# First block's attention with the values of two heads side by side and the reciprocals of the sums spread by transposes

## The chip, the core and the metric

The kernel runs on one core of one Trainium2 chip. The metric is the device time of one execution in microseconds (us), as the median of several. A core has a matrix engine (TensorE, PE in the profile; PEld are its weight loads), a vector engine (VectorE, DVE), a scalar engine (ScalarE, ACT), GpSimd (POOL) and an engine that issues transfers (SyncE, SP). Each engine works through its own queue in order, and they wait for each other through semaphores.

## What is computed

Two blocks, one after the other, on an input of 256 rows by 1024. The first is a recurrent layer, an MLP, an attention layer and another MLP. The second is a layer with a neighbourhood attention and two convolution branches. The change is in the attention of the first block alone. Cut to what matters:

```python
q, c, qi, ki, wi = jnp.split(h @ w_in, ATT_IN_SPLITS, axis=-1)
c = rms_norm(c, kv_norm_g)
...
_, idx = lax.top_k(score, topk)            # 64 of 256 keys for each query
logits = jnp.einsum('bqhc,bqkc->bqhk', q_lat_b, c_sel) + bias
p = jax.nn.softmax(logits, axis=-1)        # 16 heads
o_lat = jnp.einsum('bqhk,bqkc->bqhc', p, c_sel)
o = jnp.einsum('bshc,hcv->bshv', o_lat, w_uv).reshape(B, S, H_ATT * D_V)
return o @ w_o
```

## The kernel before, in words

**Staging.** Activations are kept transposed, features on the 128 partitions and 256 rows of the sequence on the free axis. Every weight is split into a high part (`wh`, made by ACT in `highs`, L276) and a low part (`wl`, made by DVE in `lows`, L283), and each activation too (`xh`, `xl`; here `oh`, `ol`). A product is three matmuls for each 128 of the inner dimension (L316, L318, L320): high with high, low with high, high with low. The logits, the exponentials and the values are plain fp32. For those the profile has two records for each matmul of the program (transposes have one).

**Attention.** The 256 queries are two blocks of 128. The first sees keys 0 to 127, the second all 256, so a head has 128 + 256 = 384 columns of logits (`SPANS`). Selection is a mask that GpSimd adds to the position bias (`bm`). Heads come in 8 pairs `m`, heads 2m and 2m+1. The loop over `k` is a software pipeline, written out by hand for each engine in its own function, and its order sets the order of every queue:

- `tensor_logits` (L1133, PE): the two heads of a pair side by side in rows 0 to 63 and 64 to 127 of the array.
- `vector_logits` (L1275, DVE): adds the mask and bias out of PSUM and finds the row's extreme, four instructions with four reads of the accumulator for a pair.
- `scalar_exp` (L1392, ACT): exponentials in place, the sum of each row as a by-product into `SM`.
- `tensor_flip` (L1142, PE): three 128x128 transposes for a head, so that keys come to the partitions; `scalar_flip` (L1385, ACT) copies them into `pt0` or `pt1`.
- `tensor_values` (L1153 to L1155, PE): for each head three matmuls whose stationary operand is a 128x128 piece of `pt` and whose moving operand is the head's 64 columns of values `VV`. The result has queries on the partitions.
- `vector_values` (L1281, L1286, DVE): reciprocal of the pair's four columns of sums, and the product into `os`.
- `tensor_outputs` (L1162, PE): two transposes bring heads to the partitions; `scalar_outputs` (L1397, ACT) makes `oh`, `vector_outputs` (L1292, DVE) makes `ol`.

Pair m has its logits in step m, flips and values in step m + 1, and outputs in step m + 2. Between these PE does products that don't depend on them: the second half of the query projections (`QSTEPS`, 12 matmul groups or 24 in a step) and then parts of the output projection (`tensor_wo`). In a step ACT makes one high part when `n` of `QSTEPS` is even (steps 0, 1, 3 and 5), DVE one low part in each of steps 0 to 7.

## Time and profile before

| | |
|---|---|
| median of 3 runs | 850.02 us (849.93 to 850.28) |
| the profiled execution | 849.28 us, span of the core 847.5 us |
| TensorE busy | 842.2 us, 99% of the span |
| VectorE busy | 647.2 us, 76% |
| ScalarE busy | 505.9 us, 60% |
| the loop over pairs | about 311.8 to 353.3 us of the span |

The span is the stretch that the profile shows; 1.8 us of the profiled execution lie outside it. The busy time of an engine is an average over stages and tells nothing of a single wait. Matmul records overlap, so PE's busy share can be full while it is not at its peak; what a group of matmuls costs is read from the start of its first record to the start of what follows.

### The profile page before, as it was taken

Reading aid. Unit: us, or ns where it says so; the run is one execution under the profiler, and the core shown is the slowest. Engines: PE = TensorE matmul, PEld = TensorE weight load, DVE = VectorE, ACT = ScalarE, POOL = GpSimd, SP = SyncE. Lnnn points to the kernel's source line nnn. Section 1 sums busy time; section 2 is a strip of 40 time slices with the busy share of each in tenths; the row PEclk is TensorE's granted clock in tenths of the full one; section 3 lists DMA queues with packets and bytes.
Section 4 is the critical chain, followed back from the end, with each engine's and each line's share of the span. In section 5 each row is a group of like instructions: output and inputs, shape, how many; then the busy total and the mean of one; then the engine's idle time right before and its main releaser. Section 6 shows DMA issues by size and latency. Waiting matters only on the chain.

```text
span 847.5 us, 17537 instructions
## 1 busy us (share of the span) xinstructions
PE 842.2 (99%) x7184; PEld 822.4 (97%) x7184; DVE 647.2 (76%) x1229; ACT 505.9 (60%) x925; POOL 46.8 (6%) x63
## 2 busy tenths in 40 slices
PE   8999999999999999999999999999999999999998
PEld 7999999999999998999999999999999999999998
DVE  6978668898987697586667555566699889998873
ACT  5795777774435567578878444434456685444650
POOL 0000000000000127100000000021020000000000
PEclk9999999999999999999999999999999999999999
DMA  9927868788887824177757865526564424556541
GB/s 300 347 70 224 276 213 264 265 281 267 299 263 233 283 72 140 51 247 237 208 174 217 242 207 189 189 71 154 172 198 151 148 77 142 156 170 192 170 144 50
DMA packets 162865, 164.23 MB, mean 194 GB/s; under 512 B 16816, under 2 KB 159328, under 8 KB 162528
## 3 DMA queue, kind: packets, MB, share of 16 engines
q1 hardware_dynamic: 161696, 162.05, 60.6%
q8 instruction: 57, 0.93, 0.5%
q10 hardware_dynamic: 1088, 1.05, 0.4%
q14 instruction: 24, 0.20, 0.1%
HBM read 162.01 MB, written 2.91 MB: 195 GB/s over the span
## 4 chain that ended last, share of the span: by engine, by line
PE 97%; DVE 1%; DMA 1%; ACT 0%; SPq 0%; POOL 0%; issue 0%
PE ps L316 25%; PE ps L318 25%; PE ps L320 25%; PE ps L442 3%; PE ps L1594 2%; PE ps L1592 2%; PE ps L1596 2%; PE ps L459 2%; PE ps L1685 1%; PE ps L1687 1%; PE ps L1689 1%; PE ps L1643 1%; PE ps L1654 1%; PE ps L1634 1%; DMA raw<-in_rec_w_in_dram 1%; PE ps L1133 1%
## 5 line engine op out<-in xcount | busy, mean ns | idle before, releaser
L283 DVE TENSOR_TENSOR wl<-raw,wh 128x1024 fp32r<-128x1024 f32 x256 | 309.1, 1223 | 27.1 <-ACT wh L276 27.0
L316 PE MATMUL ps<-xh,wh 128*128 128x256 f32 x1136 | 319.1, 281 | 0.0
L318 PE MATMUL ps<-xl,wh 128*128 128x256 f32 x1136 | 315.1, 277 | 0.0
L320 PE MATMUL ps<-xh,wl 128*128 128x256 f32 x1136 | 315.0, 277 | 0.0
L276 ACT ACTIVATE wh<-raw 128x1024 fp32r<-128x1024 f32 x256 | 267.1, 1051 | 73.7 <-PE ps L320 66.0
L316 PEld LDWEIGHTS ps<-xh,wh 128*128 128x128 f32 x1136 | 213.3, 188 | 3.1 <-issue 1.2
L318 PEld LDWEIGHTS ps<-xl,wh 128*128 128x128 f32 x1136 | 213.8, 188 | 0.4 <-DVE xl L384 0.2
L320 PEld LDWEIGHTS ps<-xh,wl 128*128 128x128 f32 x1136 | 213.8, 188 | 0.0
L320 PE MATMUL ps<-hh,wl 128*128 128x256 f32 x512 | 141.3, 276 | 0.0
L316 PE MATMUL ps<-hh,wh 128*128 128x256 f32 x512 | 141.3, 276 | 0.0
L318 PE MATMUL ps<-hl,wh 128*128 128x256 f32 x512 | 141.3, 276 | 0.0
L316 PEld LDWEIGHTS ps<-hh,wh 128*128 128x128 f32 x512 | 96.1, 188 | 0.0
L318 PEld LDWEIGHTS ps<-hl,wh 128*128 128x128 f32 x512 | 96.1, 188 | 0.0
L320 PEld LDWEIGHTS ps<-hh,wl 128*128 128x128 f32 x512 | 96.1, 188 | 0.0
L864 DVE TENSOR_TENSOR hl<-tmp,hh 128x256 fp32r<-128x256 f32 x64 | 27.2, 426 | 41.1 <-ACT tmp L857 40.8
L1826 DVE SCALAR_TENSOR_TENSOR ca<-up,sb_vec,ca 128x256 f32<-128x256 f32 x120 | 50.9, 479 | 0.0
L852 ACT ACTIVATE tmp<-ps 128x256 f32<-128x256 f32 x64 | 24.2, 379 | 26.2 <-PE ps L320 26.2
L884 DVE SCALAR_TENSOR_TENSOR aw<-aw,cb 128x1024 f32<-128x1024 f32 x24 | 29.3, 1220 | 6.0 <-DMA aw<-in_w_adaT_dram 5.9
L390 ACT ACTIVATE xh<-x,sb_vec 128x256 fp32r<-128x256 f32 x24 | 12.2, 510 | 34.5 <-DVE x L380 34.4
L442 PE MATMUL ps<-xg,raw 128*128 128x256 f32 x128 | 29.0, 382 | 1.5 <-DMA raw<-in_rec_w_in_dram 0.9
L442 PEld LDWEIGHTS ps<-xg,raw 128*128 128x128 f32 x128 | 23.8, 190 | 5.4 <-DMA raw<-in_rec_w_in_dram 1.7
L854 ACT ACTIVATE hh<-tmp 128x256 fp32r<-128x256 f32 x64 | 26.8, 419 | 2.0
(365 smaller groups left out, 1396.4 us busy)
## 6 DMA issues: line engine op xcount, KB each, us to landing
raw<-in_w_in_dram SPq DMA_DIRECT2D x34, 1024.0 KB, 5.4
raw<-in_mlp_up_dram SPq DMA_DIRECT2D x32, 1024.0 KB, 5.5
raw<-in_mlp_down_dram SPq DMA_DIRECT2D x32, 1024.0 KB, 7.1
aw<-in_w_adaT_dram SPq DMA_DIRECT2D x24, 512.0 KB, 4.7
raw<-in_rec_w_in_dram SPq DMA_DIRECT2D x7, 1024.0 KB, 11.6
raw<-in_att_w_in_dram SPq DMA_DIRECT2D x6, 1024.0 KB, 5.5
raw<-in_rec_w_out_dram SPq DMA_DIRECT2D x4, 1024.0 KB, 5.9
raw<-in_att_w_o_dram SPq DMA_DIRECT2D x4, 1024.0 KB, 5.0
```

The lines of the kernel that those rows point to most:

```text
L276: e.activation(parts_of(i)[0], raw_of(i), ACT.Copy).then_inc(S["wh"], 1)
L283: e.tensor_tensor(parts_of(i)[1], raw_of(i), f32(parts_of(i)[0]), op=ALU.subtract).then_inc(S["wl"], 1)
L316: e.matmul(o, H[:, first + n], xh[:, k], start=start and n == 0, stop=False)
L318: e.matmul(o, H[:, first + n], xl[:, k], start=False, stop=False)
L320: ins = e.matmul(o, L[:, first + n], xh[:, k], start=False, stop=stop and n == len(ks) - 1)
L442: ins = e.matmul(o, w[:, k], XG[:, k], start=k == 0, stop=k == 7)
L459: ins = e.matmul(o, RIW[:, n, m, j, 128 * (t % 2):128 * (t % 2) + 128], XC[:, 2 * n + j], start=j == 0, stop=j == 1)
L852: e.activation(r[:], ps[f"up{l}.{f}"], ACT.Relu).then_inc(S["hr"], 1)
L854: e.activation(HH[l][:, f], r[:], ACT.Square).then_inc(S["hh"], 1)
L864: e.tensor_tensor(HL[l][:, f], TM.of[f"s{l}.{f}"][0][:], f32(HH[l][:, f]), op=ALU.subtract).then_inc(S["hl"], 1)
L884: e.scalar_tensor_tensor(PAIR[:] if src else AW[n % 2][:], AW[n % 2][:], 1.0, CB[:, src], op0=ALU.mult, op1=ALU.mult, accum_out=(ADC if sr ...
L1826: e.scalar_tensor_tensor(CA[:, t], UP[:, t, j:j + 256], w, CA[:, t], op0=ALU.mult, op1=ALU.add).then_inc(S["cf"], 1)
```

## The change

It does four things.

1. Values: the head's 64 columns of `VV` become the stationary operand and the flipped exponentials the moving one, 256 columns for the first 128 keys and 128 for the others. The two heads of a pair go to the lower and the upper 64 partitions of one PSUM tile, so four matmuls stand in place of six, and the result has head dimensions on the partitions already. The exponentials of both heads now lie in one tile `PT` and are copied out of two PSUM banks by one ACT instruction of 768 columns.
2. Division: since queries now lie along the free axis, the reciprocals have to lie there too. DVE writes them as a tile `RR1` of 128x256 (`vector_ratios`: each of the four columns of sums is read 64 times by a stride of zero), PE transposes it with two 128x128 transposes (`tensor_ratios`), ACT copies the result into `RX` (`scalar_ratios`), and DVE multiplies (`vector_divided`) into `OT`. The transposes of the outputs are gone.
3. High and low parts of the output are made from `OT` in SBUF in place of PSUM.
4. The pipeline is a step deeper: flips of pair m in step m + 2, values, ratios and outputs in step m + 3. Both flips of a pair stand ahead of the logits. The loop has 11 steps, the pieces of the output projection beside it (`WO_BESIDE`) are laid out anew, and DVE makes its low part at the end of a step.

On DVE, in step 3, this stands before (the pair's reciprocal and product, the logits of heads 6 and 7, then the low parts; `ps` is PSUM, `small` holds the sums):

```order
L1281 RECIPROCAL small_84<-small_84 128x4
L1286 TENSOR_TENSOR os1_134<-ps2,small_84 128x256
L1275 ISA sx2_118,small_84<-ps4,bm0_131 128x128
L1275 ISA small_84 128x1
L1275 ISA sx2_118,small_84<-ps4,bm0_131 128x256
L1275 ISA small_84 128x1
L1275 ISA sx3_119,small_84<-ps5,bm1_132 128x128
L1275 ISA small_84 128x1
L1275 ISA sx3_119,small_84<-ps5,bm1_132 128x256
L1275 ISA small_84 128x1
L1292 TENSOR_TENSOR ol_136<-ps3,oh_135 128x256
L283 TENSOR_TENSOR wl0_62<-raw3_54,wh0_56 128x1024
```

and now:

```order
L1290 TENSOR_TENSOR ot0_132<-ps0,rx0_138 128x256
L1283 RECIPROCAL rr11_137<-small_84 128x256
L1276 ISA sx2_118,small_84<-ps4,bm0_130 128x128
L1276 ISA small_84 128x1
L1276 ISA sx2_118,small_84<-ps4,bm0_130 128x256
L1276 ISA small_84 128x1
L1276 ISA sx3_119,small_84<-ps5,bm1_131 128x128
L1276 ISA small_84 128x1
L1276 ISA sx3_119,small_84<-ps5,bm1_131 128x256
L1276 ISA small_84 128x1
L1294 TENSOR_TENSOR ol_135<-ot0_132,oh_134 128x256
L283 TENSOR_TENSOR wl0_62<-raw3_54,wh0_56 128x1024
```

The reciprocal is now 128x256 in place of 128x4. It still stands ahead of the four logits instructions, and so does the product, which now belongs to a pair one step older and reads `rx`, a copy that ACT makes.

On ACT, steps 3 to 4, this stands before (flips, outputs, four exponentials, the high part of a weight, and the next flip):

```order
L1385 ACTIVATE pt0_120<-ps67 128x384
L1385 ACTIVATE pt1_121<-ps67 128x384
L1397 ACTIVATE oh_135<-ps3 128x256
L1392 ACTIVATE sx2_118,small_84<-sx2_118,small_84 128x128
L1392 ACTIVATE sx2_118,small_84<-sx2_118,small_84 128x256
L1392 ACTIVATE sx3_119,small_84<-sx3_119,small_84 128x128
L1392 ACTIVATE sx3_119,small_84<-sx3_119,small_84 128x256
L276 ACTIVATE wh3_59<-raw4_55 128x1024
```

and now:

```order
L1408 ACTIVATE oh_134<-ot0_132 128x256
L1403 ACTIVATE sx2_118,small_84<-sx2_118,small_84 128x128
L1403 ACTIVATE sx2_118,small_84<-sx2_118,small_84 128x256
L1403 ACTIVATE sx3_119,small_84<-sx3_119,small_84 128x128
L1403 ACTIVATE sx3_119,small_84<-sx3_119,small_84 128x256
L276 ACTIVATE wh3_59<-raw4_55 128x1024
L1390 ACTIVATE pt_120<-ps67 128x768
L1396 ACTIVATE rx1_139<-ps2 128x256
L1408 ACTIVATE oh_134<-ot1_133 128x256
```

The copy `rx`, for which DVE's product waits, stands behind the exponentials of the step before, the high part and the wide copy `pt`; and `oh` waits for DVE's product.

The diff, cut:

```diff
@@ -1013,7 +1013,7 @@
     RT = [place(f"rt{i}", [128, 384], at=at_t) for i in range(2)]
     at_s = [ARENA]
     SX = [place(f"sx{i}", [128, 384], at=at_s) for i in range(4)]
-    PT = [place(f"pt{i}", [128, 384], at=at_s) for i in range(2)]
+    PT = place("pt", [128, 2, 384], at=at_s)
     at_t = [max(at_t[0], at_s[0])]
     SC = place("score", [128, 384], at=at_t)
     MK = place("mask", [128, 384], at=at_t)
@@ -1026,18 +1026,23 @@
     at_q = at_t[0]
     Q = place("q", [128, 8, 256], at=at_t)
     BM = [place(f"bm{i}", [128, 384], at=at_t) for i in range(2)]
-    OS = [place(f"os{i}", [128, 2, 128], at=at_t) for i in range(2)]
+    OT = [place(f"ot{i}", [128, 256], at=at_t) for i in range(2)]
     OH = place("oh", [128, 8, 256], F32R, at=[at_q])
     OL = place("ol", [128, 8, 256], F32R, at=at_t)
+    RR1 = [place(f"rr1{i}", [128, 256], at=at_t) for i in range(2)]
+    RX = [place(f"rx{i}", [128, 256], at=at_t) for i in range(2)]
     BT = place("bt", [128, 16, 256], at=[HALF])
     RQ, CVAR, CRS = TINY[:, 4:6], TINY[:, 6:8], TINY[:, 8:10]
     WI = SMALL[:, 0:16]
     M8 = [SMALL[:, 16 + 8 * i:24 + 8 * i] for i in range(2)]
-    MN, SM, RC = (SMALL[:, 32 + 32 * i:64 + 32 * i] for i in range(3))
+    MN, SM = (SMALL[:, 32 + 32 * i:64 + 32 * i] for i in range(2))
     SPANS = ((0, 128), (128, 384))
     QI_AT = {3: 1, 0: 2, 1: 3, 2: 4}
     SCORES = [2 * j + hh for j in (3, 0, 1, 2) for hh in range(2)]
     QSTEPS = (0, 0, 1, 2, 3, 4, 5, 6)
+
+    WO_BESIDE = {7: ((0, 0, 4),), 8: ((1, 0, 5),), 9: ((2, 0, 6), (0, 4, 6)),
+                 10: ((3, 0, 6), (1, 5, 7), (0, 6, 7), (2, 6, 7), (3, 6, 7))}
 
 
     def tensor_x2(e, q, name, *freed):
@@ -1136,7 +1141,7 @@
                     ins.then_inc(closing(f"lg{2 * m + i}", p[i]), 1)
 
     def tensor_flip(e, q, h):
-        p = claim(q, AUX[2 + h % 2], (S["pt"], h + 1))
+        p = claim(q, AUX[2 + h % 2], (S["pt"], h // 2 + 1))
         q.wait_ge(S["ex"], 2 * h + 2)
         for i in range(3):
             ins = e.matmul(p[:, i * 128:(i + 1) * 128], SX[h % 4][:, i * 128:(i + 1) * 128], ident, is_transpose=True)
@@ -1144,23 +1149,24 @@
 
     def tensor_values(e, q, m):
 
-        p = claim(q, AUX[m - 6], (S["os"], m + 1)) if m > 5 else main(q, (S["os"], m + 1))
+        p = claim(q, AUX[(m - 5) % 2], (S["ot"], m + 1)) if m > 4 else main(q, (S["ot"], m + 1))
         q.wait_ge(S["vv"], 4)
-        for i in range(2):
-            h, pt = 2 * m + i, PT[i]
-            cols, a, b = slice(64 * h, 64 * h + 64), slice(64 * i, 64 * i + 64), slice(128 + 64 * i, 192 + 64 * i)
-            q.wait_ge(S["pt"], h + 1)
-            e.matmul(p[:, a], pt[:, 0:128], VV[:, 0, cols], start=True, stop=True)
-            e.matmul(p[:, b], pt[:, 128:256], VV[:, 0, cols], start=True, stop=False)
-            e.matmul(p[:, b], pt[:, 256:384], VV[:, 1, cols], start=False, stop=True).then_inc(
-                closing(f"val{h}", p[:, 0:256]), 1)
-
-    def tensor_outputs(e, q, m):
-        p = claim(q, AUX[0], (S["ol"], 8)) if m == 7 else main(q, (S["ol"], m + 1))
-        q.wait_ge(S["os"], m + 1)
+        q.wait_ge(S["pt"], m + 1)
+        for blk, (lo, hi) in enumerate(((0, 256), (256, 384))):
+            for i in range(2):
+                h = 2 * m + i
+                ins = e.matmul(p[64 * i:64 * i + 64, 128 * blk:256], VV[:, blk, 64 * h:64 * h + 64], PT[:, i, lo:hi],
+                               start=blk == 0, stop=blk == 1)
+        ins.then_inc(closing(f"val{m}", p), 1)
+
+    def tensor_ratios(e, q, m):
+
+        p = ps[f"val{m}"]
+        q.wait_ge(S["rc"], m + 1)
         for blk in range(2):
-            ins = e.matmul(p[:, blk * 128:blk * 128 + 128], OS[m % 2][:, blk], ident, is_transpose=True)
-        ins.then_inc(closing(f"heads{m}", p[:, 0:256]), 1)
+            ins = e.matmul(p[:, 256 + 128 * blk:384 + 128 * blk], RR1[m % 2][:, 128 * blk:128 * blk + 128], ident,
+                           is_transpose=True)
+        ins.then_inc(closing(f"heads{m}"), 1)
 
     def tensor_wo(e, q, f, lo, hi):
 
@@ -1174,29 +1180,24 @@
         for m in range(4):
             for half in range(2):
                 tensor_q(e, q, m, half)
-        for k in range(10):
-            if 1 <= k < 9:
-                tensor_flip(e, q, 2 * k - 2)
+        for k in range(11):
+            if k > 2:
+                tensor_values(e, q, k - 3)
+            if 2 <= k < 10:
+                tensor_flip(e, q, 2 * k - 4)
+                tensor_flip(e, q, 2 * k - 3)
+            if k > 2:
+                tensor_ratios(e, q, k - 3)
             if k < 8:
                 tensor_logits(e, q, k)
-            if 1 <= k < 9:
-                tensor_flip(e, q, 2 * k - 1)
-            if k == 9:
-                tensor_wo(e, q, 0, 5, 7)
-                tensor_wo(e, q, 1, 6, 7)
-            if k > 1:
-                tensor_outputs(e, q, k - 2)
             for n, step in enumerate(QSTEPS):
                 if step == k:
                     tensor_q(e, q, 4 + n // 2, n % 2)
-            if k in (7, 8):
-                tensor_wo(e, q, k - 7, 0, k - 2)
-            if 1 <= k < 9:
-                tensor_values(e, q, k - 1)
-        tensor_wo(e, q, 2, 0, 7)
-        for f in range(3):
+            for f, lo, hi in WO_BESIDE.get(k, ()):
+                tensor_wo(e, q, f, lo, hi)
+        for f in range(4):
             tensor_wo(e, q, f, 7, 8)
-        for f in range(3, 8):
+        for f in range(4, 8):
             tensor_wo(e, q, f, 0, 8)
 
 
@@ -1275,21 +1276,22 @@
             e.tensor_tensor_reduce(SX[h % 4][:, lo:hi], ps[f"lg{h}"][:, lo:hi], BM[h % 2][:, lo:hi], 1.0, 3e38,
                                    ALU.add, ALU.min, MN[:, 2 * h + blk:2 * h + blk + 1]).then_inc(S["lg"], 1)
 
-    def vector_values(e, q, m):
-        rc = RC[:, 4 * m:4 * m + 4]
+    def vector_ratios(e, q, m):
         q.wait_ge(S["ex"], 4 * m + 4)
-        e.reciprocal(rc, SM[:, 4 * m:4 * m + 4]).then_inc(S["rc"], 1)
-        q.wait_ge(S["rc"], m + 1)
-        q.wait_ge(S["mm"], done[f"val{2 * m + 1}"])
         if m > 1:
             q.wait_ge(S["mm"], done[f"heads{m - 2}"])
-        e.tensor_tensor(OS[m % 2][:].rearrange("p a (h d) -> p (a h) d", h=2),
-                        ps[f"val{2 * m}"].rearrange("p (s d) -> p s d", s=4),
-                        rc.unsqueeze(2).to_broadcast([128, 4, 64]), op=ALU.mult).then_inc(S["os"], 1)
+        e.reciprocal(RR1[m % 2][:].rearrange("p (s d) -> p s d", s=4),
+                     SM[:, 4 * m:4 * m + 4].unsqueeze(2).to_broadcast([128, 4, 64])).then_inc(S["rc"], 1)
+
+    def vector_divided(e, q, m):
+        if m > 1:
+            q.wait_ge(S["ol"], m - 1)
+        q.wait_ge(S["rx"], m + 1)
+        e.tensor_tensor(OT[m % 2][:], ps[f"val{m}"][:, 0:256], RX[m % 2][:], op=ALU.mult).then_inc(S["ot"], 1)
 
     def vector_outputs(e, q, m):
         q.wait_ge(S["oh"], m + 1)
-        e.tensor_tensor(OL[:, m], ps[f"heads{m}"], f32(OH[:, m]), op=ALU.subtract).then_inc(S["ol"], 1)
+        e.tensor_tensor(OL[:, m], OT[m % 2][:], f32(OH[:, m]), op=ALU.subtract).then_inc(S["ol"], 1)
 
     def vector_attention(e, q):
         vector_latent(e, q)
@@ -1302,24 +1304,26 @@
         e.tensor_scalar(MK[:], SC[:], -2e38, -NEG, op0=ALU.is_ge, op1=ALU.mult).then_inc(S["mk"], 1)
         q.wait_ge(S["mk"], 1)
         e.scalar_tensor_tensor(MK[:], cc("causal"), -1.0, MK[:], op0=ALU.mult, op1=ALU.max).then_inc(S["mk"], 1)
-        for k in range(10):
+        for k in range(11):
+            if k > 2:
+                vector_divided(e, q, k - 3)
+            if 2 <= k < 10:
+                vector_ratios(e, q, k - 2)
             if k < 8:
                 vector_logits(e, q, 2 * k)
                 if k == 0:
                     vector_q(e, q, 1)
                 vector_logits(e, q, 2 * k + 1)
-            if k > 1:
-                vector_outputs(e, q, k - 2)
-            if k < 8:
-                lows(e, q, at["q5"] + k + 1)
+            if k > 2:
+                vector_outputs(e, q, k - 3)
             if k == 0:
                 vector_q(e, q, 2)
                 vector_q(e, q, 3)
             for n, step in enumerate(QSTEPS):
                 if step == k and n % 2:
                     vector_q(e, q, 4 + n // 2)
-            if 1 <= k < 9:
-                vector_values(e, q, k - 1)
+            if k < 8:
+                lows(e, q, at["q5"] + k + 1)
         for f in range(8):
             q.wait_ge(S["mm"], done[f"wo{f}"])
             x_add(e, q, 2, f, ps[f"wo{f}"])
@@ -1378,11 +1382,18 @@
             q.wait_ge(S["mm"], done[f"vv{n}"])
             e.activation(VV[:, n // 2, 512 * (n % 2):512 * (n % 2) + 512], ps[f"vv{n}"], ACT.Copy).then_inc(S["vv"], 1)
 
-    def scalar_flip(e, q, h):
-        q.wait_ge(S["mm"], done[f"flip{h}"])
-        if h > 1:
-            q.wait_ge(S["mm"], done[f"val{h - 2}"])
-        e.activation(PT[h % 2][:], ps[f"flip{h}"], ACT.Copy).then_inc(S["pt"], 1)
+    def scalar_flip(e, q, m):
+
+        q.wait_ge(S["mm"], done[f"flip{2 * m + 1}"])
+        if m:
+            q.wait_ge(S["mm"], done[f"val{m - 1}"])
+        e.activation(PT[:], PAIR[:].rearrange("p (b c) -> p b c", b=2)[:, :, 0:384], ACT.Copy).then_inc(S["pt"], 1)
+
+    def scalar_ratios(e, q, m):
+        q.wait_ge(S["mm"], done[f"heads{m}"])
+        if m > 1:
+            q.wait_ge(S["ot"], m - 1)
+        e.activation(RX[m % 2][:], ps[f"val{m}"][:, 256:512], ACT.Copy).then_inc(S["rx"], 1)
 
     def scalar_exp(e, q, h):
         for blk, (lo, hi) in enumerate(SPANS):
@@ -1393,19 +1404,19 @@
                          accum_out=SM[:, at_sum:at_sum + 1]).then_inc(S["ex"], 1)
 
     def scalar_outputs(e, q, m):
-        q.wait_ge(S["mm"], done[f"heads{m}"])
-        e.activation(OH[:, m], ps[f"heads{m}"], ACT.Copy).then_inc(S["oh"], 1)
+        q.wait_ge(S["ot"], m + 1)
+        e.activation(OH[:, m], OT[m % 2][:], ACT.Copy).then_inc(S["oh"], 1)
 
     def scalar_attention(e, q):
         scalar_latent(e, q)
         for m in range(4):
             highs(e, q, ahead(f"q{m}")[0])
-        for k in range(10):
-            if 1 <= k < 9:
-                scalar_flip(e, q, 2 * k - 2)
-                scalar_flip(e, q, 2 * k - 1)
-            if k > 1:
-                scalar_outputs(e, q, k - 2)
+        for k in range(11):
+            if 2 <= k < 10:
+                scalar_flip(e, q, k - 2)
+            if k > 2:
+                scalar_ratios(e, q, k - 3)
+                scalar_outputs(e, q, k - 3)
             if k < 8:
                 scalar_exp(e, q, 2 * k)
                 scalar_exp(e, q, 2 * k + 1)
```

## Rows read from the trace of the kernel before

**Rows 1.** The page: busy times, TensorE's clock, and the chain that ended last.

```profile
PE 842.2 (99%) x7184; PEld 822.4 (97%) x7184; DVE 647.2 (76%) x1229; ACT 505.9 (60%) x925; POOL 46.8 (6%) x63
...
PEclk9999999999999999999999999999999999999999
...
PE 97%; DVE 1%; DMA 1%; ACT 0%; SPq 0%; POOL 0%; issue 0%
```

**Rows 2.** Timeline, PE, one step (start us, us, engine, line, operation, tiles).

```profile
336.86 0.33 PE L1153 MATMUL ps<-vv,pt 128*128 128x64 f32 x2
...
341.42 0.33 PE L1153 MATMUL ps<-vv,pt 128*128 128x64 f32 x2
...
342.70 0.50 PE L1142 MATMUL ps<-sb_con,sx 128*128 128x128 f32 x3
343.13 0.93 PE L1133 MATMUL ps<-kk,q 64*128 64x128 f32 x8
343.98 0.55 PE L1142 MATMUL ps<-sb_con,sx 128*128 128x128 f32 x3
```

**Rows 3.** Timeline, PE, second block: values of two heads.

```profile
657.46 0.66 PE L1654 MATMUL ps<-pt,v 128*64 128x128 f32 x8
657.95 0.61 PE L1654 MATMUL ps<-pt,vc 128*64 128x128 f32 x8
658.48 1.09 PE L1643 MATMUL ps<-sb_con,s 128*128 128x128 f32 x8
```

**Rows 4.** Groups by form, DVE: reciprocals and two neighbours (xcount | busy, mean ns | idle).

```profile
L1902 DVE RECIPROCAL small<-small 128x2 f32<-128x2 f32 x8 | 1.3, 158 | 0.0
L1281 DVE RECIPROCAL small<-small 128x4 f32<-128x4 f32 x8 | 1.3, 165 | 0.0
L490 DVE RECIPROCAL small<-small 128x8 f32<-128x8 f32 x1 | 0.2, 203 | 0.0
...
L488 DVE TENSOR_SCALAR small<-small 128x8 f32<-128x8 f32 x1 | 0.2, 172 | 0.3 <-ACT small L704 0.3
...
L1286 DVE TENSOR_TENSOR os<-ps,small 128x256 f32<-128x256 f32 x8 | 3.4, 425 | 5.2 <-PE ps L1155 5.0
```

**Rows 5.** Timeline, DVE, step 4 of the pairs.

```profile
330.39 0.29 DVE L1275 CUSTOM_DVE_ANT_0 sx<-ps,bm 128x128 f32<-128x128 f32 x1 [0.69 <-PE ps L1133]
...
331.51 0.08 DVE L1275 DVE_READ_ACCUMULATOR2_ANT small<- 128x1 f32 x1
331.68 0.42 DVE L1292 TENSOR_TENSOR ol<-ps,oh 128x256 fp32r<-128x256 f32 x1
332.01 1.33 DVE L283 TENSOR_TENSOR wl<-raw,wh 128x1024 fp32r<-128x1024 f32 x1
333.27 0.41 DVE L1267 TENSOR_TENSOR q<-ps,rs 128x256 f32<-128x256 f32 x1
```

**Rows 6.** Timeline, ACT, step 3; then two of its groups by form.

```profile
326.94 0.40 ACT L1392 ACTIVATE sx<-sx,small 128x128 f32<-128x128 f32 x1
...
328.70 1.04 ACT L276 ACTIVATE wh<-raw 128x1024 fp32r<-128x1024 f32 x1
329.64 0.47 ACT L1385 ACTIVATE pt<-ps 128x384 f32<-128x384 f32 x1
...
L2116 ACT ACTIVATE pt<-ps 128x512 f32<-128x512 f32 x16 | 8.7, 594 | 9.5 <-PE ps L1643 9.4
L1385 ACT ACTIVATE pt<-ps 128x384 f32<-128x384 f32 x16 | 7.7, 488 | 9.0 <-PE ps L1142 8.9
L1397 ACT ACTIVATE oh<-ps 128x256 fp32r<-128x256 f32 x8 | 3.0, 381 | 4.2 <-PE ps L1162 4.2
```

**Rows 7.** Timeline, PE: the two halves of q4, and the last transposes.

```profile
312.88 0.28 PE L318 MATMUL ps<-xl,wh 128*128 128x256 f32 x1
...
315.38 0.28 PE L320 MATMUL ps<-xh,wl 128*128 128x256 f32 x1
...
353.12 0.38 PE L1162 MATMUL ps<-sb_con,os 128*128 128x128 f32 x2
```

More of the change, by code:

```diff
@@ L93, in hybrid_two_block_kernel @@
         "y yh yl eb silu hr hh hsq hl dn ada cnd qi ki wt rq wi c csq cvar crs ch cl rt sc sel mk kk vv q bm lg "
[1 row of a table removed]
-        "sa scz cgt cv by bb bz byz ybh ybl cf lsum lc lsq lacc lnv lnr rsl ly lt lq ych ycl "
[1 row of a table added]
+        "sa scz cgt cv by bb bz byz ybh ybl cf lsum lc lsq lacc lnv lnr rsl ly lt ych ycl "
         "lg2 ex2 pt2 rc2 nm2 bh yam yah yal gt mg mt mh ml fx"
```

2 rows, old and new, of the table S are left out of this document.

## The prediction

> **What bounds the kernel now.** I read the page first. PE is busy for 842.2 of 847.5 us, 97% of the chain that ended last is PE's, and the granted clock is at full speed in all slices [rows 1]. So the time is PE's queue from end to end, and only two things can change it: what PE's own instructions take, and waits that do not exist today. Next I read PE's timeline of one step of the loop over pairs. The reader is to see there that each group starts where the former ends, with no idle time noted: six matmuls of values from 341.42 to 342.70, a flip, the logits from 343.13 to 343.98, the other flip [rows 2]. A step takes 4.56 us, from the values at 336.86 to the next at 341.42 [rows 2]. DVE and ACT follow PE: DVE's logits wait 0.69 us for PE each time [rows 5]. Last I read DVE's and ACT's timelines, because the change moves work onto them.
>
> **What the change saves on PE.** The values of a pair take 342.70 - 341.42 = 1.28 us [rows 2]. The new form, 64 stationary columns and two heads in two halves of the array, is not in this loop, but the second block has it: 16 records, two by two, four pairs of records with 128 moving columns in 657.95 - 657.46 = 0.49 us, the next four in 0.53 [rows 3], so 0.12 to 0.13 us for a pair of records. The new values of a pair of heads are two pairs of records with 256 columns and two with 128, together six such units: 0.74 to 0.79 us. The logits, two heads in two halves of the rows, consist of the same number of records and columns and take 343.98 - 343.13 = 0.85 us with their switch [rows 2]. I take 0.79. The saving is 0.49 us for each pair of heads. Against it stand switches of layout. Eight transposes span 1.09 us, of which the last one's own record is some 0.3, so 0.11 each [rows 3], and three flips with the switch to the logits take 0.43 [rows 2]: a switch costs 0.1 us. One more stands now ahead of the values and one behind them, and the logits are now left towards products. I charge 0.15 to 0.2 us for a step, which leaves 0.3 us for each of eight pairs, 2.5 us in all; PE's full step becomes 4.25 us. Flips (48) and the other transposes (16) keep their number. If the two heads did not overlap, the values would cost 1.5 us and all of this would be lost; rows 3 speak against it.
>
> **What it adds: one term decides.** DVE's reciprocal goes from 128x4 to 128x256. No row shows that size. The bounds: from below, a DVE instruction of 256 columns, 0.43 us [rows 4]. From above, reciprocals by their own rows: 158 ns at 2 columns, 165 at 4, 203 at 8, while a tensor_scalar of 8 columns takes 172 [rows 4]. From 2 to 8 columns that is 45/6 = 7.5 ns a column, where ordinary instructions gain 1.2 (1.33 us at 1024 columns, 0.41 at 256 [rows 5]). From 4 to 8 it is 9.5. So R, the time of one reciprocal, is 158 + 254 x 7.5 = 2.06 us, at most 165 + 252 x 9.5 = 2.56, at least 0.43. The evidence is thin: one record of 203 ns carries the slope, and 165 at 4 columns would fit ordinary speed. I still take R = 2.05, because the steep slope is in instructions of the very same operation. The Trainium skill, "VectorE: DVE Perf Modes", section "First, the fixed hardware budget", says that a reciprocal is an iterated divide with a repeat count of 8; read as 8 cycles of its 0.96 GHz a column it would give an estimate of 2.3 us for R and by the sum below about 858 us. The trace's 7.5 ns a column agrees with it nearly.
>
> **Where R lands.** DVE's own work for a step would be the product 0.34, R, four logits instructions 1.12, low part of the output 0.34, a projection every other step 0.17, the low part of a weight 1.26 [rows 5]: 5.2 us against PE's 4.25. But a longer loop is closed through ACT. Reciprocal, then the first logits instruction, then ACT's four exponentials, its high part, the wide copy `pt`, the copy `rx`, then DVE's product, and the next reciprocal behind it. In numbers: R less an overlap of 0.08, 1.97; first logits instruction 0.30 [rows 5]; four exponentials 328.70 - 326.94 = 1.76; `pt` of 768 columns from 488 ns at 384 and 594 at 512, so 0.83 ns a column and 0.81 us, 0.70 from start to start; `rx` 0.38 by the 381 of `oh`, the same shape from PSUM [rows 6]; product 0.34; two handovers of 0.03. Sum 5.5 us, and 0.94 more (329.64 - 328.70 [rows 6]) in steps with a high part. PE cannot run ahead of it: its logits wait for DVE's of the step before, its transposes for the reciprocal, and its values for `pt`.
>
> **The sum.** Reciprocal of pair 0 starts: the last matmul of q4 ends at 315.38 + 0.28 = 315.66 [rows 7]; DVE then makes q4 (0.34), the low part (1.26), the logits of step 1 (1.12), the low part (1.26) [rows 5], so 319.7 us, no sooner than PE's logits of step 2. From there to the reciprocal of pair 6 are six rounds, two of them (steps 3 and 5) with a high part: 6 x 5.5 + 2 x 0.94 = 34.9, so 354.6. It ends at 356.65. PE, which waits for it, then does two transposes (0.22), the 24 products beside step 9 and the values of pair 7 (0.88 with the switch). Products take (315.38 - 312.88)/22 = 0.1136 us each [rows 7], so 2.73. The transposes of pair 7 start near 360.5, where today the last ones start at 353.12 [rows 7]: 7.4 us later. Behind them PE has 141 products of the output projection left, today 150: 9 x 0.1136 = 1.0 us less. Net 6.4 us, less at most 0.2 for rounding of handovers: I say 6.3. The low part of pair 7 is ready some 2 us before the products that use it, so that adds nothing. Behind the loop PE's queue is unchanged and full, so the delay is passed to the end whole. The profiled execution would go from 849.28 to 855.6 us; it is 0.7 below the median of 850.02, against which I forecast 850.0 + 6.3 = 856.3 us. Each 0.1 us of R is worth 0.7 us, seven reciprocals in line.
>
> **What I cost at nothing.** The reciprocal of the last pair and the two passes from `OT`: in steps 9 and 10 they lie beside PE's products. `RX` and `OT` as such: ACT and DVE have the time when R is small. GpSimd's bias additions are made for a pair while DVE is at the one before; should DVE's longer instruction hold GpSimd up, I allow up to 2 us in all, which the steeper case below holds. PE's waits are spread over six rounds, some 1.5 us in each, so I expect no fall of the clock, as there is none now [rows 1].
>
> **Rivals.** *The reciprocal runs at the pace of other DVE instructions* (R = 0.43). The loop is then 3.9 us, 4.8 with a high part, against PE's 4.25; some 0.3 us of waiting are left, the PE saving of 2.5 stands, 847.6 us. For it: 165 ns at 4 columns and one sole record at 8. It decides below R of about 1.1 us, where what the rounds add equals what PE saves. The Trainium skill, the same page, section "The TRN2 errata — SBUF-src ops pay a fixed extra latency per instruction", has a cycle table with 58 cycles and one for each element for VectorE; taken for the reciprocal that is an estimate of 0.33 us and this rival's time, and no row of a reciprocal above 8 columns is there to refuse it. *In between* (R from 0.7 to 1.4, say because only a start-up is slow): the loop eats what PE saves, 849 to 851.5, no change. *Steeper or with contention*: R = 2.56 by the slope from 4 to 8, or GpSimd and DVE hold each other up: 3.5 us more, 860. *The heads don't overlap in the array*: with the slow reciprocal only 0.4 us more, since PE waits anyway; with the fast one 850 to 854. Its entry in rows 3 is so clear that I give it 2 in 100.
>
> **Numbers.** Slow reciprocal, R from 1.8 to 2.3, 70 in 100, by itself 853.5 to 858.5. Steeper or contention 8 (858.5 to 861). Fast 16, in between 6. A measurement of this kernel tells about 0.2%, 1.7 us, from no change: faster takes 13 from the fast case, same gets 3 + 6, slower the rest, 78. The range from 849.0 to 859.5 holds the slow case, half of the steeper one and the one in between, 80 in 100; it leaves out the fast one.
>
> **What would show it.** Reciprocals of 128x256 at 2.0 to 2.1 us; their starts 5.5 and 6.4 us apart; PE idle ahead of the logits for DVE, ahead of the transposes for the reciprocal and ahead of the values for `pt`, some 9 us in all between 320 and 361; the values at 0.79 us with records two by two; the last transposes near 360.5. The forecast is wrong if the reciprocal takes 0.43 us, and off by size if the rounds are set by something else than ACT's queue.

## The result, and the profile after

The changed kernel takes 856.94 us in the median of four executions (856.56 to 857.46); the kernel before took 850.15 us beside it (849.93 to 850.99). The ratio is 1.0078, with a 95% interval of 1.0063 to 1.0093: it is slower by 6.8 us. The forecast was 856.3. The profiled execution is the slowest of the four, 857.46 us, with a span of 855.7 us, 8.2 more than before.

The page, against [rows 1]:

```profile
PE 845.0 (99%) x7152; PEld 819.8 (96%) x7152; DVE 658.7 (77%) x1229; ACT 508.6 (59%) x925; POOL 46.9 (5%) x63
...
PE 91%; DVE 5%; ACT 2%; issue 1%; DMA 1%; POOL 0%; ACTq 0%; DVEq 0%
```

PE is still busy for 99% of the span, but of the chain that ended last DVE and ACT now have 7%, where they had 1%. DVE gained 11.5 us of work. The timeline of DVE shows where, against [rows 5] (start us, us; in brackets the idle time before and who ended it):

```profile
334.09 1.42 DVE L283 TENSOR_TENSOR wl<-raw,wh 128x1024 fp32r<-128x1024 f32 x1
335.57 0.42 DVE L1290 TENSOR_TENSOR ot<-ps,rx 128x256 f32<-128x256 f32 x1
335.91 1.74 DVE L1283 RECIPROCAL rr<-small 128x256 f32<-128x256 f32 x1
...
338.96 1.75 DVE L283 TENSOR_TENSOR wl<-raw,wh 128x1024 fp32r<-128x1024 f32 x1
341.71 0.43 DVE L1290 TENSOR_TENSOR ot<-ps,rx 128x256 f32<-128x256 f32 x1 [1.00 <-ACT rx L1396]
342.05 1.74 DVE L1283 RECIPROCAL rr<-small 128x256 f32<-128x256 f32 x1
```

The reciprocal takes 1.74 us. From 335.91 to the next at 342.05 it is 6.14 us, and the product waits 1.00 us for `rx`. ACT's timeline of the same round, against [rows 6]:

```profile
339.61 1.05 ACT L276 ACTIVATE wh<-raw 128x1024 fp32r<-128x1024 f32 x1
340.56 0.78 ACT L1390 ACTIVATE pt<-ps 128x768 f32<-128x768 f32 x1
341.25 0.36 ACT L1396 ACTIVATE rx<-ps 128x256 f32<-128x256 f32 x1
```

The last exponential starts at 339.12; high part, `pt` and `rx` follow it without a gap, and DVE's product starts 0.1 us after `rx` ends. That is the closed round of the forecast, in the order in which it was written down. It is closed through ACT where a high part is in it; in the shorter rounds, like the one that starts at 330.71, DVE's product has no idle time before it. PE's timeline, against [rows 2]:

```profile
330.21 0.87 PE L1158 MATMUL ps<-pt,vv 128*64 128x256 f32 x8 [0.16 <-ACT pt L1390]
331.02 0.88 PE L1147 MATMUL ps<-sb_con,sx 128*128 128x128 f32 x6
332.51 0.44 PE L1167 MATMUL ps<-sb_con,rr 128*128 128x128 f32 x2 [0.62 <-DVE rr L1283]
333.65 0.93 PE L1138 MATMUL ps<-kk,q 64*128 64x128 f32 x8 [0.71 <-DVE small L1276]
...
336.08 0.87 PE L1158 MATMUL ps<-pt,vv 128*64 128x256 f32 x8
...
345.67 1.05 PE L1138 MATMUL ps<-kk,q 64*128 64x128 f32 x8 [1.38 <-DVE q L1268]
...
358.59 0.44 PE L1167 MATMUL ps<-sb_con,rr 128*128 128x128 f32 x2
```

PE waits for `pt` (0.2 us in all), for the reciprocal (1.3) and for DVE's logits (1.4), the three that were named. A fourth wait was not named and is the longest single one: 1.38 us before the last logits, for the last projection `q`, which DVE makes behind the reciprocal and the logits of its step. A step from values to values is 336.08 - 330.21 = 5.87 us in place of 4.56. The last transposes stand at 358.59, where they stood at 353.12 [rows 7]: 5.5 us later. Nine products fewer stand behind them, so the loop itself costs 4.4 us.

The rest of the time is lost behind the loop, where the forecast had nothing. In the kernel before, DVE's first and last addition to `x` after the output projection, and PE's product of the row statistics (L333), which comes behind the first products of the MLP:

```profile
356.28 0.42 DVE L380 TENSOR_TENSOR x<-x,ps 128x256 f32<-128x256 f32 x1 [1.90 <-PE ps L320]
...
370.87 0.42 DVE L380 TENSOR_TENSOR x<-x,ps 128x256 f32<-128x256 f32 x1
```

```profile
373.20 0.28 PE L333 MATMUL ps<-sb_con,sqa 128*128 128x2 f32 x2
```

In the changed kernel, DVE and then PE:

```profile
363.17 0.42 DVE L380 TENSOR_TENSOR x<-x,ps 128x256 f32<-128x256 f32 x1 [2.28 <-PE ps L320]
...
375.56 0.41 DVE L380 TENSOR_TENSOR x<-x,ps 128x256 f32<-128x256 f32 x1
...
377.76 0.41 DVE L380 TENSOR_TENSOR x<-x,ps 128x256 f32<-128x256 f32 x1
```

```profile
374.87 0.28 PE L316 MATMUL ps<-xh,wh 128*128 128x256 f32 x1
...
377.56 0.39 PE L318 MATMUL ps<-xl,wh 128*128 128x256 f32 x1 [0.38 <-DVE xl L384]
...
378.77 0.38 PE L316 MATMUL ps<-xh,wh 128*128 128x256 f32 x1 [0.70 <-ACT xh L390]
...
379.72 0.35 PE L333 MATMUL ps<-sb_con,sqa 128*128 128x2 f32 x2
```

DVE needs 2.20 us for each group of the output projection (377.76 - 375.56: the addition, a low part of a weight, the low part of `x`, its squares), and 14.59 us from the first addition to the last, in both kernels. PE's first product of the MLP comes 4.4 us later than before (370.48 there), but the first addition comes 6.9 us later, since four groups now end together behind the loop in place of three. So DVE's last `xl` is too late for PE, which waits twice, and the product of the statistics stands at 379.72, 6.5 us later than before.

The windows show the clock (us from:to, busy time, PEclk the granted clock):

```profile
340.00:346.00 6.00, 3.80 (x34) 2.93 (x34) 5.00 (x14) 4.04 (x13) 3.35 (x5) 1.00 0.03 9
346.00:350.00 4.00, 4.00 (x24) 3.20 (x22) 3.94 (x12) 2.04 (x7) 1.86 (x2) 0.57 0.44 129
376.00:380.00 4.00, 2.78 (x19) 2.08 (x17) 3.42 (x7) 2.61 (x6) 0.00 (x0) 1.00 0.84 261
380.00:384.00 4.00, 4.00 (x22) 4.00 (x22) 3.47 (x5) 2.86 (x5) 0.71 (x1) 0.57 0.53 140
```

Twice, right after stretches in which PE was busy for 3.80 of 6 and 2.78 of 4 us, TensorE is granted 1.2 in place of 2.4 GHz: a mean of 0.57 over 4 us is 3.4 us at half speed. The second time the queue is full. From this product of the statistics to the next of its kind PE takes 43.53 us (379.72 to 423.25), in the kernel before 41.92 (373.20 to 415.12): the half speed cost 1.6. So the profiled execution had lost 4.4 + 2.1 + 1.6 = 8.1 us here. Farther back it loses 1.1 us between 586 and 647 us and gets 1.0 back behind it; a kernel with the attention of before shows the same loss (e5, last section), so it is not put down to the change. The three other executions have a mean clock of 1.000, where this one has 0.996; their difference of 6.8 us to the kernel before is the first two terms, 6.5, and 0.3 left over. That they lost the same two terms is inferred: only one execution has a trace.

### The profile page after: what moved, and what is told of

Its sections match the earlier page's. It is cut to its first block, busy times and chain, and to the rows that moved or that the text cites. A ratio compares the mean times of both kernels' runs of the same rounds, so it can differ in the third digit from the quotient of the medians.

```text
span 855.7 us, 17472 instructions
## 1 busy us (share of the span) xinstructions
PE 845.0 (99%) x7152; PEld 819.8 (96%) x7152; DVE 658.7 (77%) x1229; ACT 508.6 (59%) x925; POOL 46.9 (5%) x63
## 4 chain that ended last, share of the span: by engine, by line
PE 91%; DVE 5%; ACT 2%; issue 1%; DMA 1%; POOL 0%; ACTq 0%; DVEq 0%
PE ps L316 24%; PE ps L318 24%; PE ps L320 24%; PE ps L442 2%; PE ps L1605 2%; PE ps L1607 2%; PE ps L1603 2%; PE ps L459 2%; PE ps L1696 1%; PE ps L1698 1%; PE ps L1700 1%; DVE wl L283 1%; PE ps L1665 1%; PE ps L1654 1%; PE ps L1645 1%
```

## The experiments

Four questions were open: whether the reciprocal is all that makes the loop slow; whether the rounds close through ACT; what the loss behind the loop is; and what the reciprocal costs by size. The last runs put the answers together.

**e1: the reciprocal stays small.** The changed kernel with DVE's spreading done by a multiplication.

```diff
-        e.reciprocal(RR1[m % 2], <4 columns of SM, each read 64 times>)
+        e.reciprocal(rc, SM[:, 4 * m:4 * m + 4])
+        e.tensor_scalar(RR1[m % 2], <4 columns of rc, each read 64 times>, 1.0, None, op0=ALU.mult)
```

> The changed kernel, but the reciprocal is taken of the four columns of sums (128x4) and a tensor_scalar by 1.0 spreads it to 128x256. Theory A, the 1.74 us reciprocal sets the rounds through ScalarE's queue: it becomes 0.17 + 0.35 us, the rounds fall from 5.2 and 6.1 us to 3.9 and 4.9, PE hardly waits between 320 and 360 us (under 1.5 us, now about 8), and the time is 847.5 to 849.0 us. Rival B, the deeper pipeline and the copy rx cost by themselves: it stays at 854 us or more.

Measured: 852.02 us (850.83 to 854.62), ratio 1.0032 (1.0020 to 1.0045) to 849.58. PE's timeline:

```profile
321.62 0.87 PE L1158 MATMUL ps<-pt,vv 128*64 128x256 f32 x8
...
325.87 0.87 PE L1158 MATMUL ps<-pt,vv 128*64 128x256 f32 x8
...
353.19 0.44 PE L1167 MATMUL ps<-sb_con,rr 128*128 128x128 f32 x2
...
374.31 0.35 PE L333 MATMUL ps<-sb_con,sqa 128*128 128x2 f32 x2
```

In the loop the theory holds: steps of 4.25 us, to the hundredth what the forecast gave PE alone, two waits of PE left (0.80 us for `q`, 0.42 for DVE's logits), and the last transposes at 353.19 in place of 358.59. But the total is 3 us over the range that was expected. PE's MLP starts a microsecond earlier than before, and the statistics 1.1 us later: the same loss of 2.1 us behind the loop as in the changed kernel. So that loss has nothing to do with the reciprocal, nor with a late loop. Of the seven executions four have a mean clock of 0.998 (spans 849.0, 851.2, 852.2, 852.7) and three of 1.000 (849.0, 849.7, 850.2); the profiled one is at half speed for 3.4 us around 376, behind these waits. From its statistics to the next of their kind it takes 44.78 us (to 419.09) in place of 41.92; the half speed explains 1.7 of these 2.9 us, the rest is a slower pace of the products with no wait between them (last section).

**e2: `rx` ahead of `pt` on ACT.** Nothing else is changed.

```diff
         for k in range(11):
-            if 2 <= k < 10:
-                scalar_flip(e, q, k - 2)
             if k > 2:
                 scalar_ratios(e, q, k - 3)
+            if 2 <= k < 10:
+                scalar_flip(e, q, k - 2)
+            if k > 2:
                 scalar_outputs(e, q, k - 3)
```

> The changed kernel, with ScalarE's small copy rx put ahead of its wide copy pt in each step; nothing else. Theory A, the round runs through ScalarE: it loses the 0.7 us of pt until VectorE's own work (4.9 us a step) holds it, so rounds of about 4.9 and 5.4 us in place of 5.2 and 6.1, some 2.5 us less in all, 854.0 to 855.0 us. Rival C, VectorE's own work or PE's waits for the reciprocal already set the pace: no change, 856.5 to 857.3.

Measured: 854.61 us (854.06 to 857.32), ratio 1.0067 (1.0055 to 1.0080). DVE's timeline:

```profile
334.72 1.74 DVE L1283 RECIPROCAL rr<-small 128x256 f32<-128x256 f32 x1
...
339.82 0.42 DVE L1290 TENSOR_TENSOR ot<-ps,rx 128x256 f32<-128x256 f32 x1 [0.31 <-ACT rx L1396]
340.17 1.74 DVE L1283 RECIPROCAL rr<-small 128x256 f32<-128x256 f32 x1
```

The round with a high part is 5.45 us in place of 6.14, the wait for `rx` 0.31 in place of 1.00: exactly the 0.69 by which `rx` stands earlier. The last transposes stand at 356.47, 2.1 us earlier, and of the 6.8 us by the medians 5.0 are left. That is inside the range expected if the round runs through ACT. The ratios alone would not show it, since their intervals overlap: two of the five executions have a mean clock of 0.998 and spans of 854.5 and 855.5 us, where the other three have 852.3 to 852.7. The trace does. The round closes through ACT where a high part is in it; in the others (5.06 us here, 5.20 in the changed kernel) DVE's product does not wait for `rx`, and DVE's own queue is the limit.

**e3: three groups beside the loop.** The output projection is divided as in the kernel before: groups 0, 1 and 2 beside the loop, five behind it.

```diff
-                 10: ((3, 0, 6), (1, 5, 7), (0, 6, 7), (2, 6, 7), (3, 6, 7))}
+                 10: ((1, 5, 7), (0, 6, 7), (2, 6, 7))}
...
-        for f in range(4):
+        for f in range(3):
             tensor_wo(e, q, f, 7, 8)
-        for f in range(4, 8):
+        for f in range(3, 8):
```

> The changed kernel, but with three groups of the output projection begun beside the loop (0, 1, 2) in place of four, as in the kernel before. Theory D, behind the loop VectorE needs 2.2 us for each of the eight groups and four groups that end together leave PE 2.7 us of products for only four more: PE then waits about 2 us at the start of the next MLP and the clock falls for 3.4 us there. With three groups these waits go, at the price of 0.7 us of waiting for the last low part: 853.5 to 855.5 us. Rival: PE's waits at 377 us come from the late loop itself and stay: 856.5 to 857.5.

Measured: 853.75 us (853.48 to 854.10), ratio 1.0049 (1.0036 to 1.0062). PE's timeline:

```profile
358.46 0.44 PE L1167 MATMUL ps<-sb_con,rr 128*128 128x128 f32 x2
...
378.17 0.28 PE L333 MATMUL ps<-sb_con,sqa 128*128 128x2 f32 x2
```

The loop ends where it ended (358.46), DVE's additions start 1.8 us earlier (361.36), both waits of PE are gone, and the statistics come 1.55 us earlier. It is not the whole 2.1, because the fourth group had covered something: with twelve products in place of 33 between the last transposes and those that read the last `oh` and `ol`, PE's weight loads wait 0.27 us for each of the two, and three products there take 1.03 us in the starts (360.01 to 361.04) in place of 0.34. The ratio falls by 0.0029, 2.5 us, a microsecond more than the trace says; the intervals allow both. Its profiled execution is granted half speed in the loop, near 346, and has a span of 851.7, as much as its sister executions with a mean clock of 1.000 (851.7 to 852.1): in the loop, where PE waits for DVE anyway, half speed shows no cost in the span.

**e4: the kernel before with a large reciprocal that nobody reads.** In `vector_values`, ahead of the small one.

```diff
+        e.reciprocal(RQX[m % 2], <4 columns of SM, each read 64 times>)
         e.reciprocal(rc, SM[:, 4 * m:4 * m + 4]).then_inc(S["rc"], 1)
```

> The kernel before, with a reciprocal of 128x256 into a tile that nobody reads, ahead of its own small one in each of the eight steps. VectorE's own work for a step goes from about 3.5 to 5.2 us against PE's 4.56. Theory A in its general form (1.7 us more on VectorE can't be hidden in this loop): PE waits about 0.6 us a step from step 2 on, 854 to 856 us. Rival (only the closed round through rx makes it costly): under 851.5 us.

Measured: 853.70 us (853.00 to 855.24), ratio 1.0050 (1.0037 to 1.0063). DVE and PE:

```profile
334.70 1.74 DVE L1282 RECIPROCAL rqx<-small 128x256 f32<-128x256 f32 x1
...
339.73 1.74 DVE L1282 RECIPROCAL rqx<-small 128x256 f32<-128x256 f32 x1
```

```profile
326.71 0.41 PE L1163 MATMUL ps<-sb_con,os 128*128 128x128 f32 x2 [0.62 <-DVE os L1289]
```

Eight of these instructions alone cost 4.1 us, just under the range expected and far over the rival's 851.5: DVE's round becomes 5.0 to 5.4 us by its own work, more than PE's 4.56, and PE waits for `os` in six of the eight steps, here 0.62 us. The last transposes stand at 356.85. With e1 this shows the cause of the loss in the loop from both sides: without the large reciprocal they stand where they stood (353.19 against 353.12), and the large reciprocal alone moves them by 3.7 us in a loop that has neither `rx` nor the deeper pipeline.

**e5: the reciprocal by size.** The kernel before with reciprocals of 2 to 128 columns and multiplications of 1, 32 and 223 at the head of DVE's queue, all reading one column by a stride of zero. The edit adds, in `vector_mixer`:

```diff
+        for n in (2, 4, 8, 16, 32, 64, 128):
+            e.reciprocal(SQX[:, at_p:at_p + n], NEGH[:, 0:1].to_broadcast([128, n]))
```

> The kernel before, with reciprocals of 128x2, 4, 8, 16, 32, 64 and 128, read with a stride of zero, and tensor_scalars of 128x1, 32 and 223 at the start of VectorE's queue, where it waits for the input. If every column costs the reciprocal 6.3 ns (1.744 us at 256), 128 columns take 0.94 us, 64 take 0.54 and 32 take 0.34, while 32 columns of tensor_scalar take 0.18. If instead the cost began only above some size, or came from the copies' three-dimensional pattern in the changed kernel, 128 columns would take 0.3 us.

Measured in one execution of 850.4 us, the groups of DVE (the number after the bar: busy us, mean ns):

```profile
L564 DVE RECIPROCAL sqx<-negh 128x128 f32<-128x128 f32 x1 | 0.9, 895 | 0.0
...
L564 DVE RECIPROCAL sqx<-negh 128x64 f32<-128x64 f32 x1 | 0.5, 495 | 0.0
...
L564 DVE RECIPROCAL sqx<-negh 128x32 f32<-128x32 f32 x1 | 0.3, 296 | 0.0
L567 DVE TENSOR_SCALAR tmp<-negh 128x223 f32<-128x223 f32 x1 | 0.3, 270 | 0.0
...
L564 DVE RECIPROCAL sqx<-negh 128x8 f32<-128x8 f32 x1 | 0.2, 174 | 0.0
...
L564 DVE RECIPROCAL sqx<-negh 128x4 f32<-128x4 f32 x1 | 0.2, 157 | 0.0
```

From 64 to 128 columns it is 400 ns, 6.25 ns a column; from 128 to 256, with the 1744 ns of the changed kernel, 849 ns, 6.6 a column. Up to 8 columns the time stays between 157 and 174 ns, so the slope can't be read there. The one record of 8 columns takes 174 ns here; the kernel's own, on which the forecast's slope hung, takes 203 in this run too. The expectation's rival, 0.3 us for 128 columns, is refuted.

**e8: e1 and e3 together**, and **e9: `rx` first as well** (the edits of e1, e3, and e2).

> Both remedies together: the reciprocal of 128x4 with a tensor_scalar that spreads it, and three groups of the output projection beside the loop. Theory: what is left of the change is PE's saving of about 0.3 us for a pair, less 0.8 us of waiting for q7, 0.4 for a free bank and 0.6 for the last low part: 848.5 to 850.0 us on this chip, no clear difference from before. Rival: if the deeper pipeline has a price of its own, or PE's saving is not there, 851 or more.

> As the run before it, and ScalarE's copy rx ahead of its copy pt. The rounds through ScalarE lose 0.7 us, so VectorE's q7 comes earlier and the wait of 0.8 us ahead of the last logits goes: 848.0 to 849.5 us, about 0.5 us under the run without it. If that wait has another cause: the same as without it.

Measured, beside 27 executions of the kernel before (850.08 us): e8 849.76 us (849.33 to 850.90), ratio 1.0001 (0.9992 to 1.0010); e9 848.46 us (847.73 to 848.94), ratio 0.9982 (0.9973 to 0.9990). All executions have a mean clock of 1.000. PE's timeline of e9:

```profile
352.04 0.44 PE L1167 MATMUL ps<-sb_con,rr 128*128 128x128 f32 x2
...
371.74 0.28 PE L333 MATMUL ps<-sb_con,sqa 128*128 128x2 f32 x2
```

e8 has its statistics at 373.12, where the kernel before has 373.20; e9 at 371.74, 1.5 us earlier, and the median follows with 1.6. So e9 is better than both kernels, by a little: of the 2.5 us that PE was to save in the loop 1.5 arrive. The last transposes stand 1.1 us earlier than before, with nine products (1.0 us) more ahead of them, so 2.1 us are saved in the loop, in steps of 4.26 us; 0.7 are lost again to the wait for the last `oh` and `ol`, as in e3. In e8 PE still waits 1.2 us at two places in the loop, for `q` (0.81) and for DVE's logits (0.42); with `rx` first those two are gone. By the medians e9 gains 1.3 us on e8, more than the 0.5 expected.

**e7: PE spreads the ratios itself**, with three groups as in e3, and **e10: `rx` first as well.** The tile `RR1` goes; four matmuls with 64 stationary columns, all the same column of the small reciprocal, stand in place of the two transposes, directly behind the values.

```diff
+            for i in range(2):
+                ins = e.matmul(p[64 * i:64 * i + 64, 256 + 128 * blk:384 + 128 * blk],
+                               RC[:, 4 * m + 2 * blk + i:4 * m + 2 * blk + i + 1].to_broadcast([128, 64]), ident,
+                               start=True, stop=True)
```

> Three groups beside the loop, and no spread tile at all: four matmuls with the column of reciprocals as a stationary operand of 64 equal columns and the identity moving, right behind the values, in place of two transposes. VectorE loses the 0.35 us of spreading, PE pays 4 pairs of records (0.44 us) for two transposes (0.22): 0.2 us more for a pair on PE. 848.5 to 850.5 us: a little better than the tensor_scalar if VectorE still sets the pace, a little worse (1 us) if PE does.

> The kernel of the run e7 (the reciprocals of the sums stay a column of four; four products of TensorE with the identity spread them; three groups of the output projection beside the loop) with ScalarE's copy of the spread ratios put ahead of its copy of the flipped exponentials. In e7 the part beside the loop and behind it costs TensorE 2.5 us less of gaps than in the changed kernel, and the last transposes lie where they lay before. Theory (the round through ScalarE still sets VectorE's and with it TensorE's step): the earlier copy takes 0.5 to 1.6 us off, as it did in e9 against e8 (1.3 us): 848.4 to 849.6 us. Rival (TensorE is already full in e7's loop, 39.92 us busy in 40 us, so no order of copies can give it anything): 849.8 to 850.2 us. Second rival: a difference of kernels of under 1 us is set by the stretch from 600 to 645 us, where every changed kernel so far came back 0.8 to 1.2 us late whatever was done in the loop; then it falls on e7's time as well.

Measured: e7 850.05 us (849.26 to 851.38), ratio 1.0001 (0.9992 to 1.0010); e10 849.95 us (849.31 to 850.61) beside 849.95, ratio 1.0002 (0.9993 to 1.0011). PE's timeline of e7:

```profile
330.45 0.87 PE L1158 MATMUL ps<-pt,vv 128*64 128x256 f32 x8
331.16 0.61 PE L1168 MATMUL ps<-sb_con,small 128*64 128x128 f32 x8
331.69 0.87 PE L1147 MATMUL ps<-sb_con,sx 128*128 128x128 f32 x6
...
334.96 0.87 PE L1158 MATMUL ps<-pt,vv 128*64 128x256 f32 x8
```

A step is 4.51 us, 0.25 more than in e9 and nearly the 4.56 of before: the spreading takes 331.69 - 331.16 = 0.53 us of the engine that sets the end. DVE has 26.17 us of work between 320 and 360 in place of the 29.14 of e8, and it buys nothing. In e10 the first rival of its expectation holds: PE is full in the loop (39.92 of 40 us in both), and an earlier `rx` gives it at most 0.2 us. The second rival, that differences under 1 us are made in the stretch from 600 to 645 us, names something real: e10 does lose 1.1 us there against the trace of the kernel before. But its "every changed kernel so far" is not so: e3 doesn't lose it, and e5, whose attention is that of the kernel before, does.

## Why the prediction was right, and where it was not

**The mechanism of the loop was right.** The reciprocal of 128x256 is slow and decides the sign (e1, e4); the round closes through ACT where a high part is in it (e2), while in the others DVE's own work is just as long; PE waits for the three things named, and for `q`. The formula for the round, with the measured 1.744 us in place of 2.05, gives 5.2 and 6.14 us; the starts of the reciprocals in the changed kernel (319.12, 324.63, 330.71, 335.91, 342.05, 347.25, 352.87) are 5.51, 6.08, 5.20, 6.14, 5.20 and 5.62 apart. The two rounds of 5.51 and 5.62 are longer than the formula; in both ACT's `pt` waits for PE (0.26 and 0.29 us), the second time right behind the stretch at half speed.

**The term R was mis-sized: 1.744 us, not 2.05.** It was inside its bounds, 0.43 and 2.56. The slope of 7.5 ns a column hung on the one record of 203 ns at 8 columns; e5 shows 6.25 to 6.6 from 64 columns up. Seven reciprocals in line make 7 x 0.306 = 2.1 us too much. The last transposes came at 358.59, not at 360.5, and the loop cost 4.4 us, not 6.3; the first reciprocal also stood 0.6 us earlier than forecast, and the two longer rounds took about as much back. Neither reading of the Trainium skill that the prediction weighed fits ("VectorE: DVE Perf Modes", sections "First, the fixed hardware budget" and "The TRN2 errata — SBUF-src ops pay a fixed extra latency per instruction"): the estimate of 2.3 us from a repeat count of 8 is a third too high, the 0.33 us from the cycle table a fifth of what was measured.

**The step "Behind the loop PE's queue is unchanged and full, so the delay is passed to the end whole" failed.** It counted PE's products behind the loop (141 against 150) and not DVE's. The queue there was not unchanged: four groups end together in place of three, and DVE, at 2.20 us for each of eight groups, is then the longer chain. That is 2.1 us, shown in the changed kernel and in e1 and taken away in e3, where 0.7 us of another wait come in its place. The two errors cancel, -1.9 and +2.1. That 856.3 came so near to 856.94 is therefore luck; that the change is slower by several microseconds, and through the reciprocal, is not.

**"I expect no fall of the clock" failed for the profiled execution and held for the medians.** The waits of 0.6 to 1.4 us in the loop and two of 0.4 and 0.7 behind it came before stretches at half speed, which cost 1.6 us in the profiled execution where the queue was full. Three of four executions show a mean clock of 1.000.

**PE's saving was right in size.** The values are 0.80 us with their switch (331.02 - 330.21; forecast 0.79 without it), and PE's full step is 4.25 us in e1 and 4.26 in e9, as forecast. The heads do overlap. In the whole kernel e9 shows 1.5 us of the 2.5: 2.1 were saved in the loop, and 0.7 went to the wait for the last `oh` and `ol`, which the forecast put at nothing, rightly only as long as four groups cover it.

**PE idle of 9 us was not seen:** in the windows from 330 to 350 PE is busy for 15.6 us, so idle for 4.4. The last transposes are 5.5 us late: 4.4 idle, 1.0 for nine products more ahead of them and 1.7 for the stretch at half speed near 347, which leaves 1.6 for what was saved. Without the slow stretch PE would for the most part have been idle for longer, not done sooner: e3's executions at full clock are no shorter. **GpSimd:** the reciprocal does not hold it up, but the low parts beside GpSimd's additions last 1.42 and 1.75 us, where the forecast's 1.26 from start to start stands for a duration of 1.33 [rows 5]. In the round through ACT this is covered; in the rounds of 5.20 us it is part of DVE's own sum.

**A small slip in the rivals.** The fast rival's 847.6 us is 850.0 - 2.5 + 0.3 = 847.8 by its own terms; nothing hangs on it.

## What to carry to other kernels

A reciprocal is not an ordinary vector instruction: compute it on the few distinct values and spread the result with a copy or a multiplication. When an edit delays a stretch, the queue of every engine behind that stretch has to be counted, not only that of the engine that sets the end: how many tiles become ready at once, and how long each takes downstream. And a gain on the bounding engine arrives only if the round of small dependent steps around it is shorter than its step. Where that round is the limit, the copy that closes it belongs first in its queue (e2, e9); where it isn't, the order gives nothing (e10).

## What the runs showed of the hardware

A reciprocal on DVE takes 157 ns at 4 columns, 296 at 32, 495 at 64, 895 at 128 and 1744 at 256, when a multiplication of 223 columns takes 270 ns. Both read their source by a stride of zero.

GpSimd and DVE slow each other when both work from SBUF. GpSimd's addition of 128x128 is 0.46 us alone and 1.44 beside DVE's low part of a weight, in the kernel before as well, and that of 128x256 goes from 0.73 to 0.98 beside `ol`, which now reads SBUF alone. It looks as if one waits until the other is done, rather than both being slower throughout: in the changed kernel DVE's low parts that start at 334.09 and 338.96, inside such an addition, end 1.08 and 1.09 us behind its end (334.43 and 339.62), and such a low part alone takes 1.22.

In the profiled execution of the changed kernel TensorE was granted 1.2 in place of 2.4 GHz twice, for 3.4 us each. In the 6 us before the first it had worked for 3.80, with a longest wait of 1.38; in the 4 us before the second for 2.78, with waits of 0.38 and 0.70. Whether an execution gets there differs from one to the next: in e1 four of seven show it in their mean clock, in e9, which lacks those waits, none of eleven.

Two executions can differ by a microsecond with neither a wait nor a change of clock. PE between the same two products of the second block, in the kernel before and then in e5:

```profile
577.86 0.27 PE L1610 MATMUL ps<-sb_con,sqb 128*128 128x128 f32 x1
...
637.31 0.27 PE L1610 MATMUL ps<-sb_con,sqb 128*128 128x128 f32 x1
```

```profile
578.18 0.27 PE L1618 MATMUL ps<-sb_con,sqb 128*128 128x128 f32 x1
...
638.69 0.27 PE L1618 MATMUL ps<-sb_con,sqb 128*128 128x128 f32 x1
```

That is 59.45 and 60.51 us for the same instructions. Of the eleven traces, three have the shorter time (before, e3, e4), the others the longer. PE is busy throughout at a granted clock of 1.00; from 600 to 630 us its products stand 0.113 us apart in the one and 0.118 in the other. What decides between the two paces is open. So a difference of a microsecond between two spans is no evidence by itself, and the readings here rest on the place in the trace where the time is lost.
